# Moving the first block's residual to tokens-as-partitions in a fused two-block transformer kernel

## The reference, cut to what matters

```python
# first block (DEPTH = 1)
a = rms_norm(x, norm_mix);   h = x + stick_breaking_mixer(a, sb_w_qkv, sb_w_o)   # o @ sb_w_o: 2048 x 2048
h = h + square(relu(rms_norm(h, norm_mlp) @ mlp_w1)) @ mlp_w2                    # 2048 -> 8192 -> 2048
x = rms_norm(h, final_norm)
# second block
h = rms_norm_2(x, pre_mix_g);  z = h @ w_in          # q, k, v (1024 each) and u (1024)
m = concat(chunked_attention(q, k, v), multiscale_pool(u)) @ w_o
x = x + rms_norm_2(m, post_mix_g)
h = rms_norm_2(x, pre_ffn_g);  up = causal_dwconv(h @ w_up)      # 2048 -> 2 x 5632
x = x + rms_norm_2((gelu(up[:, :5632]) * up[:, 5632:]) @ w_down, post_ffn_g)
```

## Time and profile before

| | us |
|---|---|
| time, median of three runs | 2145.47 |
| the three runs | 2144.96, 2145.47, 2149.38 |
| time of the profiled execution | 2149.53 |
| its span, first to last instruction | 2147.8 |
| PE busy | 2129.4 (99%) |
| PEld busy | 1849.0 (86%) |
| POOL busy | 241.4 (11%) |
| HBM read | 395.55 MB, 185 GB/s over the span |

### The profile page before, as it was taken

One profiled execution on the slowest core, in us unless ns is written; L12 is line 12 of the kernel. 1 busy time (PEld: TensorE's weight loads), 2 busy tenths in 40 slices (PEclk: granted clock), 3 DMA queues, 4 the chain that ended last, 5 costly groups with the idle time before them and its releaser, 6 DMA issues.

```text
span 2147.8 us, 28157 instructions
## 1 busy us (share of the span) xinstructions
PE 2129.4 (99%) x11700; PEld 1849.0 (86%) x11700; DVE 1285.9 (60%) x1335; ACT 1064.6 (50%) x1198; POOL 241.4 (11%) x135
## 2 busy tenths in 40 slices
PE   8999999999999999999999999999999999999998
PEld 7888888888888888888888888888888888888886
DVE  6555556655555565565669655576666644566655
ACT  6554554545334443444554544455455433555553
POOL 2000001100000000000224000032222100222211
PEclk9999999999999999999999999999999999999999
DMA  8555545564655655665555555545555656556553
GB/s 278 162 173 176 176 167 186 176 205 169 210 191 183 196 185 193 177 205 189 190 196 191 179 175 182 181 149 176 193 185 180 209 193 194 178 178 206 196 198 114
DMA packets 207472, 399.50 MB, mean 186 GB/s; under 512 B 12400, under 2 KB 15600, under 8 KB 207088
## 3 DMA queue, kind: packets, MB, share of 16 engines
q1 hardware_dynamic: 207056, 395.60, 56.7%
q10 hardware_dynamic: 288, 2.10, 0.2%
HBM read 395.55 MB, written 2.10 MB: 185 GB/s over the span
## 4 chain that ended last, share of the span: by engine, by line
PE 98%; DVE 1%; ACT 0%; DMA 0%; issue 0%; SPq 0%; DVEq 0%; ACTq 0%
PE ps L1338 98%; DMA raw<-in_sb_w_qkv_dram 0%; PE ps L1341 0%; DVE raw L1236 0%; DVE Wl L1026 0%; DVE E L1065 0%; ACT E L864 0%; ACT E L862 0%; ACT T L960 0%; ACT zs L857 0%; DVE QK L1215 0%; ACT E L860 0%; ACT L862 0%; ACT Wh L814 0%; DVE aHL L1188 0%
## 5 line engine op out<-in xcount | busy, mean ns | idle before, releaser
L1026 DVE TENSOR_TENSOR Wl<-raw,Wh 128x1024 fp32r<-128x1024 f32 x745 | 920.0, 1255 | 618.2 <-ACT Wh L814 617.1
L1338 PE MATMUL ps<-aHL,Wh 128*128 128x512 f32 x3328 | 1164.6, 394 | 8.3 <-DVE Wl L1022 6.3
L814 ACT ACTIVATE Wh<-raw 128x1024 fp32r<-128x1024 f32 x745 | 768.7, 1054 | 608.7 <-PE ps L1338 604.6
L1338 PE MATMUL ps<-aHL,Wl 128*128 128x256 f32 x3328 | 931.8, 280 | 0.0
L1338 PEld LDWEIGHTS ps<-aHL,Wh 128*128 128x128 f32 x3328 | 624.5, 188 | 150.8 <-DVE aHL L1016 6.3
L1338 PEld LDWEIGHTS ps<-aHL,Wl 128*128 128x128 f32 x3328 | 629.3, 189 | 0.4
L1338 PE MATMUL ps<-hid,Wh 128*128 128x512 f32 x1024 | 355.1, 391 | 0.0
L1338 PE MATMUL ps<-hid,Wl 128*128 128x256 f32 x1024 | 286.7, 280 | 0.0
L1338 PEld LDWEIGHTS ps<-hid,Wh 128*128 128x128 f32 x1024 | 191.5, 187 | 42.0
L1338 PE MATMUL ps<-Wh,hid 128*128 128x512 f32 x704 | 217.6, 389 | 0.0
L1338 PEld LDWEIGHTS ps<-hid,Wl 128*128 128x128 f32 x1024 | 193.5, 189 | 0.0
(11 more groups left out here) (173 smaller groups left out, 1290.4 us busy)
## 6 DMA issues: line engine op xcount, KB each, us to landing
raw<-in_mlp_w_dram SPq DMA_DIRECT2D x256, 512.0 KB, 4.4
raw<-in_w_up_dram SPq DMA_DIRECT2D x176, 512.0 KB, 3.8
raw<-in_sb_w_qkv_dram SPq DMA_DIRECT2D x95, 512.0 KB, 4.5
raw<-in_w_down_dram SPq DMA_DIRECT2D x88, 512.0 KB, 4.4
raw<-in_w_in_dram SPq DMA_DIRECT2D x64, 512.0 KB, 4.5
raw<-in_sb_w_o_dram SPq DMA_DIRECT2D x32, 512.0 KB, 4.5
raw<-in_w_o_dram SPq DMA_DIRECT2D x32, 512.0 KB, 3.8
xT<-in_x_dram SPq DMA_DIRECT2D x8, 256.0 KB, 8.1
```

Of the source, the lines that this page charges most:

```text
L814: e.activation(Wh[:, i % NW, :], rawv[:, i % NRAW, :], ACT.Copy).then_inc(st["hi"][0], 1)
L1026: e.tensor_tensor(Wl[:, i % NW, :], rawv[:, i % NRAW, :], Wh[:, i % NW, :].bitcast(F32), ALU.subtract).then_inc(st["lo"][0], 1)
L1338: return e.matmul(o, l, r, start=start, stop=stop, skip_group_check=True)
```

## The change

The residual of the first block is kept with tokens as partitions (`xN`, 128 x 2 x 2048), loaded as such from a second copy of x in eight transfers behind pieces 30 to 37. `sb_w_o` and `mlp_w2` become kind "N". Their result is added to `xN` in one DVE operation per 128 tokens; for `mlp_w2` it is multiplied by r2 squared there, so that "relu" needs no r. Squares are summed per token by ACT's accumulator ("row_squares"), and "row_norm" and "row_pair" get r from these sums without matmuls. "turn" makes feature tiles by eight plain transposes for each four tiles, with the gain applied as PSUM is read. "mixed_tiles", "turn_x3", "gained_squares" and the first block's "spread" are gone. The gains of the final norm and of `post_mix_g_2` are loaded as rows, one broadcast transfer each. `wide` matmuls (of `ones` and `r_a`) now stand behind the last "turn" ahead of `mlp_w1` and ahead of the first `mlp_w1` piece of chunks two and three, besides the one in `w_up_2`. "row_norm" for r6 stands behind piece 8 of `w_up_2`, its spread two pieces later; the spread of r4 two pieces behind "row_pair". Behind the last `w_o_2` strip the kept rows, already multiplied by the gain as a row, are added to `xN` with r ("add_rows", for the first 512 features in two halves), and the four turns stand behind pieces 0, 1, 3 and 5 of what follows. In the diff below the semaphore increments of the engines' lines are left out.

```diff
-    def evac_residual(s4, gain_name=None, more=None):
+    def evac_rows(s4, gain_name=None, scaled=False, more=None):
         def f(s, k):
...
+            added = [done("rows_added") for t in range(2)]
+            step("add_products", s4=s4, set=s, mm=k, x_rows=x_rows[-1], factor=st["r2sq"] if scaled else None, done=added)
+            free[f"set{s}"] = [added[1]]
+            if gain_name == "mlp":
+                row_squares(s4, added)
+                later(2, lambda: turn(s4, "mlp", added, wide=s4 == 3))
+            if gain_name == "pre2":
+                sq = row_squares(s4, added)
+                def gained():
+                    g = [done("rows_gained") for t in range(2)]
+                    step("gain_rows_x", n=s4, need=sq, row=st["final_row"], done=g)
+                    row_squares(s4, g, gained=True)
+                    later(2, lambda: turn(s4, "pre2", g))
+                later(1, gained)
...
-        strip("sb_w_o", s4 * STRIP, ALL8, "oHL1", oHL_tiles, evac_residual(s4, "mlp"))
+        strip("sb_w_o", s4 * STRIP, ALL8, "oHL1", oHL_tiles, evac_rows(s4, "mlp"), kind="N")
...
             if at + j == 0:
-                after(i + 4, r_job("r2", "b", "r_b"))
+                after(i + 3, lambda: row_norm(squared=True))
+            elif j == 0:
+                p.pieces[i]["wide"] = True
...
-                  evac_residual(s4, "in2" if c == 2 else None, load_bias if c == 2 and s4 == 3 else None), koff=2 * at)
+                      evac_rows(s4, "pre2" if c == 2 else None, True, load_bias if c == 2 and s4 == 3 else None), kind="N",
+                      koff=2 * at)
...
-    after(u0 + 4, rms_pair)
+    after(u0 + 4, row_pair)
...
+            add_rows(0)
+            tiles(0)   
             for n in (1, 2, 3):
-                later(n, lambda n=n: tiles(4 * n))
+                later(2 * n - 1, lambda n=n: tiles(n))
+            for n in range(4):
+                later(2 * n + 1, lambda n=n: row_squares(n, [added[n][-1]] * 2))
...
-                    after(i + 10, r_job("r6", "b", "r_b"))
+                    after(i + 8, lambda: row_norm(spreads="r6"))
...
-                after(i + 6, turn_x3(0))
-                after(i + 8, turn_x3(1))
...
+                elif k == "norm_x":
+                    for t in range(2):
+                        e.activation(xN[:, t, cs], xN[:, t, cs], ACT.Copy, scale=cols["a"][:, t:t + 1])
+                elif k == "add_products":
+                    for t in range(2):
+                        e.wait_ge(*st["mm"][t])
+                        if st["factor"]:
+                            e.scalar_tensor_tensor(out=xN[:, t, cs], in0=ps[st["set"]][:, t, :], scalar=cols["b"][:, t:t + 1],
+                                                   in1=xN[:, t, cs], op0=ALU.mult, op1=ALU.add)
+                        else:
+                            e.tensor_tensor(xN[:, t, cs], xN[:, t, cs], ps[st["set"]][:, t, :], ALU.add)
...
+                    e.scalar_tensor_tensor(out=T0[:, :, :], in0=T1[:, :, :], scalar=0.0, in1=T1[:, :, :], op0=ALU.max,
+                                           op1=ALU.mult)
...
+                elif k == "turn":
+                    for i in range(4):
+                        j = 4 * st["n"] + i
+                        if st["halves"] and i in (0, 2):
+                            e.wait_ge(*st["halves"][0 if i == 0 else -1])
+                        for t in range(2):
+                            m = tp(turned_tile(st["set"], i)[:, t * 128:(t + 1) * 128], xN[:, t, j * 128:(j + 1) * 128])
+                    if st["wide"]:
+                        mm(ps[st["set"]][:, 1, 0:TOK], ones[:, :], r_a[:, :], True, True)
```

More of the change, by code:

```diff
@@ L128, in rms_pair, with turn @@
         second = dict(root=done("rms_root"), rec=done("rms_rec"), sq=done("rms_rec"), prod=done("rms_rec"), r=done("rms_r"))
[L129 to L143, removed]
+        both, diag = done("rms_r"), done("rms_diag")
+        step("row_pair", need=st["rows_sq"], zs_free=list(free["zs"]), ident=ident, total=total, mean=mean, first=first,
+             square=square, moved=moved, mean2=mean2, second=second, both=both, diag=diag)
+        st["r3c"], st["r4c"], st["diag"] = first["r"], both, diag
+        after(p.at + 2, lambda: spread("r4", "r_b"), ahead=True)
+    def turn(n, gain_name, need, wide=False):
+        s = side_set()
+        turned = [done("rows_turned") for i in range(3)]
+        hi = [done("tile_hi") for j in range(4)]
+        lo = [done("tile_lo") for j in range(4)]
+        step("turn", n=n, set=s, gain=gain_name, need=[*need, ident, *free[f"set{s}"]], halves=None, wide=st["r1"] if wide else None,
+             turned=turned, hi=hi, lo=lo)
+        free[f"set{s}"] = [lo[3]]
+        tile_hl[4 * n:4 * n + 4] = lo
     def spread(name, row):
@@ L244, in plan_program @@
         after(first["v", g] + 12, values(g, 1))
-    def evac_residual(s4, gain_name=None, more=None):
+    def evac_rows(s4, gain_name=None, scaled=False, more=None):
         def f(s, k):
[L248 to L261, removed]
+            added = [done("rows_added") for t in range(2)]
[9 more added lines that the diff above has]
+                    step("gain_rows_x", n=s4, need=sq, row=st["final_row"], done=g)
+                    st["final_used"] = g[1]
+                    row_squares(s4, g, gained=True)
+                    later(2, lambda: turn(s4, "pre2", g))
+                later(1, gained)
             if more:
-                more(s, k)
+                more(s, k[1])
         return f
     for s4 in range(4):
-        strip("sb_w_o", s4 * STRIP, ALL8, "oHL1", oHL_tiles, evac_residual(s4, "mlp"))
+        strip("sb_w_o", s4 * STRIP, ALL8, "oHL1", oHL_tiles, evac_rows(s4, "mlp"), kind="N")
     hid_tiles = [None] * 24
@@ L351, in pool_piece @@
         p.pieces.append(dict(src=("pool_w_2", "groups", 2 * j, 0), shape=4, mov="oHL2", kt=4 * j, tiles=pool_tiles,
-                             kind="P", first=True, last=True, evac=evac_mix(j)))
+                             kind="P", first=True, last=True, evac=evac_mix(j), wide=False))
     for g in range(2):
@@ L419, in f @@
             total, mean, root = done("row_total"), done("rms_mean"), done("rms_root")
[L420 to L438, removed]
@@ new lines, in f, with add_rows @@
+            rec, sq2, prod, r = done("rms_rec"), done("rms_rec"), done("rms_rec"), done("rms_r")
+            step("mixed_norm", set=s, sq=sq, warm=warm, total=total, mean=mean, root=root, rec=rec, sq2=sq2, prod=prod, r=r)
+            st["bank0"] = kept[0]
+            added = {}
+            def add_rows(n):
+                added[n] = [done("rows_added", 2) for h in range(2 if n == 0 else 1)]
+                step("add_rows", n=n, need=[r, *st["kept", n], st["x2", n]],
+                     done=added[n])
@@ new lines, in tiles @@
+            def tiles(n):
+                turned = [done("rows_turned") for i in range(3)]
+                hi = [done("tile_hi") for j in range(4)]
+                lo = [done("tile_lo") for j in range(4)]
+                step("turn", n=n, set=s, gain="ffn", need=[ident, st["bank0"]], halves=added[n], wide=None, turned=turned,
+                     hi=hi, lo=lo)
+                tile_hl[4 * n:4 * n + 4] = lo
+                st["bank0"] = lo[3]
+                free[f"set{s}"] = [lo[3]]
+                if n < 3:
+                    add_rows(n + 1)
+                if n == 0:
+                    step("keep_last", set=s, row=st["mixed_row"], kept=kept[1])
@@ L580, in split, with load_rows @@
             load(i + NRAW)
+    x_rows = []
+    def load_rows(c):
+        x_rows.append(done("x_rows", 16))
+        step("load_rows", c=c, done=x_rows[-1])
+    for c in range(8):
+        after(30 + c, lambda c=c: load_rows(c))
     def load_x_rest(i):
@@ L1527, in _ @@
             tensor_program(eng)
-_INS = ["sb_w_qkv", "sb_w_o", "mlp_w1", "mlp_w2", "w_in_2", "pool_w_2", "w_o_2", "w_up_2", "w_down_2", "post_ffn_g_2"]
-_GAINS = ["norm_mix", "norm_mlp", "final_norm", "pre_mix_g_2", "post_mix_g_2", "pre_ffn_g_2", "pool_scale_2"]
+_INS = ["sb_w_qkv", "sb_w_o", "mlp_w1", "mlp_w2", "w_in_2", "pool_w_2", "w_o_2", "w_up_2", "w_down_2", "final_norm", "post_mix_g_2",
+       "post_ffn_g_2"]
+_GAINS = ["norm_mix", "norm_mlp", "pre_mix_g_2", "pre_ffn_g_2", "pool_scale_2"]
 def kernel(**inputs):
```

334 lines of the change are left out of this document (159 added, 175 removed).

## The result

| | before | after |
|---|---|---|
| time, median of five runs each, us | 2149.38 | 2138.08 |
| lowest and highest | 2144.96, 2150.16 | 2136.89, 2138.60 |
| profiled execution, us | 2149.53 | 2138.2 |
| its span, us | 2147.8 | 2136.5 |

The ratio is 0.9953, with a 95% interval from 0.9938 to 0.9967: faster by 0.47%. The five times of before form two groups, two near 2145 and three near 2150; after lies in one. So the size of the difference depends on the draw: from the lower group of before the change takes 7.1 us (0.33%), from the upper one 11.6 us (0.54%).

What follows compares the result with a forecast made beforehand. The prediction took the length of PE's own instruction stream (busy 99%) as the bound. From the profiled 2149.5 us, kind -8.4, side work -0.1, stall -1.0, pace -4.5 and slow pieces +1.0 gave -13.0: 2136.5 us, range 2134.3 to 2141.2.

Steps and rivals of the forecast that it cites:

- The kind of piece: In `sb_w_o` and `mlp_w2`, 160 pieces go from T (2.773 us) to N (2.721): 8.4 us less.
- Side work: Between PE's pieces: 11.6 us removed, 11.5 added by eleven turns at 0.93 and three `wide` products; 0.1 less.
- The stall: PE's wait between the last `w_o_2` piece and `w_up_2`: from 6.4 to about 5.4 us, 1.0 less.
- No turn came late: Rival, chance 0.05: new low halves late on DVE, PE waits at three turns, up to 1 us each; 2138 to 2139.5.
- The spread of r6: In `w_up_2`'s first chunk: its diagonal comes on time, so 84 pieces become fast, 4.5 us less.
- N pieces and transposes leave T slow, and a float32 product of 256 columns that is on time makes it fast: Rule read from PE's timeline for T pieces' two paces, 0.053 us a piece apart; basis of the pace terms.
- the 1.0 us that I added for slow pieces: 20 slow T pieces before the first float32 product: 2 in `mlp_w1`, 7 in `w_in_2`, up to 11 in `w_up_2`.
- one stretch stays slow: Rival, chance 0.20: `mlp_w1`'s first chunk slow behind transposes and `wide`, +2.5 us, or `w_up_2`'s first chunk, +4.5.
- The slow pace everywhere: Rival, chance 0.05: `mlp_w1`, `w_in_2` and `w_up_2`, 338 pieces, run at 2.827 us, 18.0 us; time 2153.5.

Runs made afterwards that it cites:

- Experiment 8: The changed kernel with every transpose of the turns issued twice: 2147.18 us, 9.1 more than the changed kernel.
- experiment 5: The kernel before with r6's sums one piece earlier and its spread where it was: 2145.98 us, all 11 runs between 2145.46 and 2146.98.
- experiment 6: The changed kernel with r6's norm and spread both right behind piece 10 of `w_up_2`, so PE waits: 2139.66 us; three of eleven runs 2143.39 to 2143.93.
- experiment 7: The kernel before with only `sb_w_o` and `mlp_w2` made kind N (output wrong): 2142.53 us; with `wide` products at chunks two and three too: 2139.33 us.
- experiment 4: The changed kernel without the turn's `wide` product, the three others with 128 columns instead of 256: 2142.35 us, 8.2 more than with 256.
- experiment 3: The changed kernel without the two `wide` products at chunks two and three of `mlp_w1`: 2141.09 us, 3.0 more than the changed kernel.

## Why the prediction was right, and where it was off

**The kind of piece**: right. 2.721 us a piece in the first block too, 8.4 us, in `mlp_w2` 130.63 and 108.84 us for 48 and 40 pieces. The pieces' own paces in the rows, 13.4 ns a matmul above its columns, decided. The 2.5 ns that the Trainium skill ("TensorE: Matmul & The Clock Gate", "Back-to-back issue gap") gives for an isolated warm matmul is not what this stream shows.

**Side work**: nearly right. I took a turn as half of "turn_x3", 0.93; it is 0.88, so eleven of them cost 0.6 less than forecast. Experiment 8 prices the transpose at 0.11 us. The 275 ns of the Trainium skill (same page, "Part 4: PE-mode transpose") is the length of one here too (0.27 us), and no distance between two.

**The stall**: right, 5.45 for 5.4. The chain is the one worked out: r, two half rows, transposes, two high halves, one low half. No turn came late.

**The spread of r6**: right in what it gave. 4.5 us of pace came back in the profiled execution, and the two groups of times are gone; experiment 5 shows the same in the kernel before. The reason was too simple. I read the earlier trace rows as "late, so slow" and put the two groups down to a diagonal that is sometimes on time. Four traces have a late one: the kernel before is slow behind it, experiment 6 and both kernels of experiment 7 are fast (in the second the product takes 0.34 us instead of 0.24). In all nine traces in which it was on time the stretch is fast.

**What failed** is the step "N pieces and transposes leave T slow, and a float32 product of 256 columns that is on time makes it fast". Two of its three parts are wrong. Transposes did not leave T slow: behind the last turn of `w_in_2` it was fast, so 3 pieces were slow there and not 7, and in `w_up_2` one and not up to 11; the 1.0 us that I added for slow pieces is 0.3. And the product does not always make it fast: right behind eight transposes it left 46 pieces slow, +2.4 us. That was the rival "one stretch stays slow", in the place I had named, with 2.5 us as its price; 0.20 was too little for a case that no row covered. A further 0.5 us came up to `sb_w_o`, where no piece was changed: the first strips fell on the slow pace in this profiled execution (pieces 3 to 13 at 2.83 us) and on the fast one in the other (2.77).

The balance against -13.0: slow `mlp_w1` +2.4, start +0.5, cheaper turns -0.6, fewer slow pieces -0.7, stall and rounding +0.1, together -11.3. That the forecast came within 1.7 us of the profiled execution is in part luck: +2.9 of misses stand against -1.2. So is the closeness of 0.47% to the forecast 0.42%, which was meant against a median of 2145.5 and was measured against one of 2149.38, the upper group.

**The slow pace everywhere** did not come, but experiment 4 shows that this rival was real: products of half the length leave 160 pieces slow and take 8.2 us, nearly all that the change of kind brings. The change needed its two `wide` products at chunks two and three of `mlp_w1` (experiment 3), and the one in `w_up_2` its full length (experiment 4); the one in the turn harmed it.

## What to carry to other kernels

Where PE is busy 99% of the time, read the distance between starts, stretch by stretch, and compare stretches of the same instructions: a uniform 2% in one of them hides in every busy share. Count matmuls, not only columns: here the same columns in 12 instead of 16 instructions were 2% less time, though nothing separates the count from the kind of piece, which changed with it. After every edit beside a long uniform stream, look at its pace again, since a block that is cheap by itself can set the pace of what follows; and give a product that waits for another engine a piece more of lead.

## What the runs showed of the hardware

A piece has 6144 columns, 2.560 us at 2.4 GHz; the granted clock was 1.00. A T piece of 16 matmuls took 2.773, an N piece of 12 took 2.721: 13.3 and 13.4 ns a matmul more than its columns, on average. The slow pace, 2.827, is 16.7 ns. The starts in the traces show where it goes. In an N stream each matmul of 512 columns starts 226.7 to 227.0 ns behind the one before, in all thirteen kernels. In a T stream the distance is 230 to 232 ns behind a matmul of 512 columns and 115 to 117 behind one of 256, 346.7 a pair; at the slow pace it is 236 to 237 and 116 to 117, 353.3 a pair. So nearly all of the loss lies behind the wider matmul. Only the T stream, whose matmuls alternate between 512 and 256 columns, has two paces.

The pace of a T stream changed only at side blocks or strips of the other kind, and it held for up to 85 pieces (236 us). Behind N pieces: slow in every case. Behind N and a float32 product of 256 columns: fast in every case; of 128 columns: slow in all three. Behind eight transposes on a slow stream: fast; behind twelve: slow. Eight or sixteen transposes and then a product: slow; a product and then eight transposes: fast. One product on time behind a fast stream: fast; two: slow. But the block alone does not tell the pace. Behind r's sums on a fast stream (four instructions of one column, on time) eight stretches were fast and four slow. Behind the 16 products of "mixed_tiles" on a fast stream four were fast and three slow; in the kernel before, the piece at 1400.11 took 2.78 us and the one at 1404.67, behind the same block, 2.81. This looks like an alignment in time that the side block's length shifts, but what is aligned with what was not found, and no rule is offered that would tell the pace ahead of a run.
